# Triangular inverse of the delta rule in 32x32 blocks on four partition groups

## The reference, cut to what matters

```python
D_MODEL = 2048
SEQ = 256
DN_HEADS = 8
DN_HEAD_DIM = 128
DN_CHUNK = 64

def chunk_gated_delta_rule(q, k, v, g, beta):
    ...
    decay = jnp.exp(jnp.where(causal, g[..., :, None] - g[..., None, :], -jnp.inf))
    k_beta = k * beta[..., None]
    v_beta = v * beta[..., None]
    a = jnp.einsum("bhncd,bhnsd->bhncs", k_beta, k) * decay
    t_mat = jnp.eye(C, dtype=jnp.float32) + jnp.where(strict, a, 0.0)
    rhs = jnp.concatenate([v_beta, k_beta * jnp.exp(g)[..., None]], axis=-1)
    sol = lax.linalg.triangular_solve(t_mat, rhs, left_side=True, lower=True, unit_diagonal=True)
    ...
```

## Time and profile before

| | us |
|---|---|
| median of 3 runs | 2566.45 (2566.37 to 2567.07) |
| the profiled execution | 2566.27 |
| its span, first to last instruction | 2564.5 |
| TensorE busy | 2543.6 (99%) |
| VectorE busy | 1674.9 (65%) |
| ScalarE busy | 1339.4 (52%) |
| DMA, mean | 184 GB/s |

### The profile page before, as it was taken

One profiled execution on the slowest core, in us unless ns is written; L12 is line 12 of the kernel. 1 busy time (PEld: TensorE's weight loads), 2 busy tenths in 40 slices (PEclk: granted clock), 3 DMA queues, 4 the chain that ended last, 5 costly groups with the idle time before them and its releaser, 6 DMA issues.

```text
span 2564.5 us, 33902 instructions
## 1 busy us (share of the span) xinstructions
PE 2543.6 (99%) x13816; PEld 2149.8 (84%) x13816; DVE 1674.9 (65%) x2150; ACT 1339.4 (52%) x1893; POOL 0.2 (0%) x4
## 2 busy tenths in 40 slices
PE   9999999999999999999999999999999999999998
PEld 7878888888888888887888888888888888888887
DVE  7686566655665566668778987555566655665565
ACT  6565554444444446568766656544554444444444
POOL 0000000000000000000000000000000000000000
PEclk9999999999999999999999999999999999999999
DMA  6544666566556555555454447554656655655654
GB/s 226 166 138 145 223 222 202 188 196 192 189 195 191 189 195 178 189 184 171 144 181 147 149 149 253 175 166 153 197 181 197 197 185 193 195 185 195 196 187 143
DMA packets 235858, 470.79 MB, mean 184 GB/s; under 512 B 8283, under 2 KB 17206, under 8 KB 234550
## 3 DMA queue, kind: packets, MB, share of 16 engines
q1 hardware_dynamic: 234950, 467.04, 55.7%
q10 hardware_dynamic: 752, 1.58, 0.2%
HBM read 462.30 MB, written 6.29 MB: 183 GB/s over the span
## 4 chain that ended last, share of the span: by engine, by line
PE 49%; DVE 1%; ACT 1%; issue 0%; DVEq 0%
PE ps L1291 10%; PE ps L1293 10%; PE ps L1292 10%; PE ps L1330 9%; PE ps L1329 5%; PE ps L1679 1%; PE ps L1362 0%; ACT WH L1911 0%; PE ps L1829 0%; PE ps L1857 0%; PE ps L1828 0%; PE ps L1856 0%; PE ps L1855 0%; PE ps L1827 0%; PE ps L1662 0%
## 5 line engine op out<-in xcount | busy, mean ns | idle before, releaser
L2663 DVE TENSOR_TENSOR WL<-Wt,WH 128x1024 fp32r<-128x1024 f32 (+1 forms) x861 | 1037.9, 1210 | 678.1 <-ACT WH L1911 630.0
L1911 ACT ACTIVATE WH<-Wt 128x1024 fp32r<-128x1024 f32 (+1 forms) x861 | 895.4, 1047 | 777.6 <-PE ps L1293 517.6
L1291 PE MATMUL ps<-WH,XT 128*128 128x512 f32 (+1 forms) x1184 | 469.6, 397 | 0.8 <-DVE WL L2663 0.5
L1293 PE MATMUL ps<-WH,XT 128*128 128x512 f32 (+1 forms) x1184 | 459.5, 388 | 0.0
L1292 PE MATMUL ps<-WL,XT 128*128 128x512 f32 (+1 forms) x1184 | 459.2, 388 | 0.0
L1291 PE MATMUL ps<-WH,HT 128*128 128x512 f32 (+2 forms) x1176 | 456.1, 388 | 1.5 <-DVE WL L2663 1.5
L1293 PE MATMUL ps<-WH,HT 128*128 128x512 f32 (+2 forms) x1176 | 451.4, 384 | 0.0
L1292 PE MATMUL ps<-WL,HT 128*128 128x512 f32 (+2 forms) x1176 | 451.0, 384 | 0.0
L1330 PE MATMUL ps<-XT,WH 128*128 128x512 f32 x960 | 336.5, 394 | 0.0
L1330 PE MATMUL ps<-HT,WH 128*128 128x512 f32 x960 | 336.5, 394 | 0.0
L1329 PE MATMUL ps<-XT,WL 128*128 128x256 f32 x960 | 266.6, 278 | 0.0
(11 more groups left out here) (424 smaller groups left out, 1922.2 us busy)
## 6 DMA issues: line engine op xcount, KB each, us to landing
Wt<-in_mlp_w SPq DMA_DIRECT2D x128, 1024.0 KB, 5.2
Wt<-in_w_up SPq DMA_DIRECT2D x64, 1024.0 KB, 5.2
Wt<-in_w_down SPq DMA_DIRECT2D x64, 1024.0 KB, 5.0
Wt<-in_w_in SPq DMA_DIRECT2D x53, 1024.0 KB, 5.1
Wt<-in_w_out SPq DMA_DIRECT2D x32, 1024.0 KB, 5.1
Wt<-in_xa_wk SPq DMA_DIRECT2D x16, 1024.0 KB, 5.1
Wt<-in_xa_wv SPq DMA_DIRECT2D x16, 1024.0 KB, 5.1
Wt<-in_xa_wq SPq DMA_DIRECT2D x16, 1024.0 KB, 5.2
```

The lines of the kernel that those rows point to most:

```text
L1291: pe.matmul(o, xh, wh, start=start, stop=False)
L1293: done = pe.matmul(o, xl, wh, start=False, stop=stop)
L1911: act.activation(m.WH[:, i % NR, 0:2 * w], m.Wt[:, slot % NW, h * 2 * w:(h + 1) * 2 * w], ACT.Copy).then_inc(*up("wsplit.a", i))
L2663: dve.tensor_tensor(m.WL[:, i % NR, 0:2 * w], m.Wt[:, slot % NW, h * 2 * w:(h + 1) * 2 * w], m.WH[:, i % NR, 0:2 * w].bitcast(F32), SUB).t ...
```

## The change

Levels 0 to 4 of the inverse work inside blocks of 32, so four 32x32 blocks of a head can lie on four partition groups, `QUARTERS`, packed in 32 columns. `small_blocks` is that view: 8 heads x 32 columns, 256 in all. For li below 5, `on_tiles` issues 8 x 4 matmuls of 32x32; masks, factor and copies are 256 columns wide. `d_blocks` adds four copies of 32x256 on ScalarE into the upper part of MI and keeps the two wide ones, which only the mask of level 32 reads. After li = 4 VectorE spreads MI and MT back to 64-wide blocks, `widen`: the 32 columns are read twice and multiplied by `own32`. That replaces ScalarE's two copies there. The yield between `d_blocks` and `d_first` goes, and the second mask moves from `d_lev2` into `d_first`.

```diff
     for s in LEVELS:
-        r, c = (i, j) if s == LEVELS[-1] else (i % 64, j[:, 0:64])
+        w = P if s == LEVELS[-1] else max(2 * s, 32)
+        r, c = i % w, j[:, 0:w]
...
+    parts.append(("ident32", (i % 32 == j[:, 0:32]) * 1.0))
     parts.append(("ident64", (i % 64 == j[:, 0:64]) * 1.0))
+    parts.append(("own32", (i % 64 // 32 == j[:, 0:64] // 32) * 1.0))
...
+QUARTERS = tuple(slice(32 * n, 32 * n + 32) for n in range(4))
+
+def small_blocks(t, part=0):
+    return t[:, 2 * part:2 * part + 2, :].rearrange("p a (e c) -> p (a e) c", e=4)
...
             p.do("d_blocks", b)
-            yield
             p.do("d_first", b)
             yield
             yield
...
     def on_tiles(name, b, li, use, left, right):
+        tiles, w = (TILES, 64) if li == 5 else (QUARTERS, 32)
         for s in freed(use):
             on.wait_ge(*s)
         for h in range(8):
-            for r in TILES:
-                done = pe.matmul(m.bank(use)[r, 64 * h:64 * h + 64], left(r, h), right(r, h), start=True, stop=True)
+            for r in tiles:
+                done = pe.matmul(m.bank(use)[r, w * h:w * h + w], left(r, h), right(r, h), start=True, stop=True)
...
     def d_left(b, li, use):
+        part = blocks if li == 5 else small_blocks
         on.wait_ge(*at("delta.v", "level", b, li))
-        on.wait_ge(*at("delta.a", "plain", b, li - 1))
+        on.wait_ge(*(at("delta.v", "plain", b) if li == 5 else at("delta.a", "plain", b, li - 1)))
...
     def d_blocks(b):
         on.wait_ge(*at("delta.v", "pairs", b))
+        for r in QUARTERS:
+            act.activation(small_blocks(MI, 2)[r, :, :], AT[r, :, r], ACT.Copy).then_inc(*up("delta.a", "blocks", b))
         for r in TILES:
-            act.activation(blocks(MT, 1)[r, :, :], AT[r, :, r], ACT.Copy).then_inc(*up("delta.a", "blocks", b))
+            act.activation(blocks(MT, 1)[r, :, :], AT[r, :, r], ACT.Copy).then_inc(*up("delta.a", "wide blocks", b))
...
     def d_first(b):
         on.wait_ge(*at("delta.a", "blocks", b))
         delta_prev(b)
-        dve.tensor_tensor(blocks(BT), blocks(MT, 1), mk("lev1"), MUL).then_inc(*up("delta.v", "level", b, 0))
+        dve.tensor_tensor(small_blocks(BT), small_blocks(MI, 2), mk("lev1"), MUL).then_inc(
+            *up("delta.v", "level", b, 0))
         on.wait_ge(*at("delta.v", "level", b, 0))
-        dve.tensor_tensor(blocks(MT), mk("ident64"), blocks(BT), SUB).then_inc(*up("delta.v", "first", b))
-
-    @named
-    def d_lev2(b, use):
+        dve.tensor_tensor(small_blocks(MT), mk("ident32"), small_blocks(BT), SUB).then_inc(*up("delta.v", "first", b))
         on.wait_ge(*at("delta.v", "qk", b, 1))
         if b == 0:
             on.wait_ge(*at("delta.v", "dl"))
-        dve.tensor_tensor(blocks(DT), blocks(MT, 1), mk("lev2"), MUL).then_inc(*up("delta.v", "level", b, 1))
+        dve.tensor_tensor(small_blocks(DT), small_blocks(MI, 2), mk("lev2"), MUL).then_inc(*up("delta.v", "level", b, 1))
...
+    def widen(dst, use):
+        ps = m.bank(use)[:, 0:256].rearrange("p (h c) -> p h c", h=8)
+        own = m.cst("own32").rearrange("p (e c) -> p e c", e=2)
+        return dve.tensor_tensor(blocks(dst).rearrange("p h (e c) -> p h e c", e=2),
+                                 ps.unsqueeze(2).to_broadcast([P, 8, 2, 32]),
+                                 own.unsqueeze(1).to_broadcast([P, 8, 2, 32]), MUL)
...
     def d_right(b, li, turned, plain=None):
+        if li == 4:
+            on.wait_ge(*at("delta.t", "plain", b, 4))
+            widen(MI, plain).then_inc(*up("delta.v", "plain", b, frees=plain))
+            on.wait_ge(*at("delta.t", "turned", b, 4))
+            widen(MT, turned).then_inc(*up("delta.v", "turned", b, frees=turned))
```

More of the change, by code:

```diff
@@ L1684, in d_lev2 @@
         on.wait_ge(*at("delta.v", "first", b))
-        on_tiles("plain", b, 0, use, lambda r, h: blocks(MT)[r, h, :], lambda r, h: ident[r, r])
+        on_tiles("plain", b, 0, use, lambda r, h: small_blocks(MT)[r, h, :], lambda r, h: ident[r, r])
     @named
     def d_left(b, li, use):
+        part = blocks if li == 5 else small_blocks
         on.wait_ge(*at("delta.v", "level", b, li))
-        on.wait_ge(*at("delta.a", "plain", b, li - 1))
-        on_tiles("left", b, li, use, lambda r, h: blocks(bts[li % 2])[r, h, :], lambda r, h: blocks(MI)[r, h, :])
+        on.wait_ge(*(at("delta.v", "plain", b) if li == 5 else at("delta.a", "plain", b, li - 1)))
+        on_tiles("left", b, li, use, lambda r, h: part(bts[li % 2])[r, h, :], lambda r, h: part(MI)[r, h, :])
     @named
     def d_right(b, li, turned, plain=None):
+        part = blocks if li == 5 else small_blocks
         on.wait_ge(*at("delta.v", "factor", b, li))
-        on.wait_ge(*(at("delta.a", "turned", b, li - 1) if li > 1 else at("delta.v", "first", b)))
+        if li == 5:
+            on.wait_ge(*at("delta.v", "turned", b))
+        else:
+            on.wait_ge(*(at("delta.a", "turned", b, li - 1) if li > 1 else at("delta.v", "first", b)))
         if plain:
-            on_tiles("plain", b, li, plain, lambda r, h: blocks(MT)[r, h, :], lambda r, h: blocks(m.E0)[r, h, :])
-        on_tiles("turned", b, li, turned, lambda r, h: blocks(m.E0)[r, h, :], lambda r, h: blocks(MT)[r, h, :])
+            on_tiles("plain", b, li, plain, lambda r, h: part(MT)[r, h, :], lambda r, h: part(m.E0)[r, h, :])
+        on_tiles("turned", b, li, turned, lambda r, h: part(m.E0)[r, h, :], lambda r, h: part(MT)[r, h, :])
     @named
@@ L2436, in d_right @@
     def d_right(b, li, turned, plain=None):
-        if plain is None:
+        if li >= 4:
             return
@@ L3459, in d_left @@
         to, src = bts[(li + 1) % 2], AT
-        if LEVELS[li + 1] < 64:
+        if LEVELS[li + 1] == 32:
+            on.wait_ge(*at("delta.a", "wide blocks", b))
             to, src = blocks(to), blocks(MT, 1)
+        elif LEVELS[li + 1] < 32:
+            to, src = small_blocks(to), small_blocks(MI, 2)
         dve.tensor_tensor(to[:, :, :], src[:, :, :], mk(f"lev{LEVELS[li + 1]}"), MUL).then_inc(
```

5 lines of the change are left out of this document (3 added, 2 removed).

## The result

The changed kernel takes 2571.1 us (median of 13 runs, 2568.75 to 2574.84) against 2566.5 (2566.35 to 2567.07): ratio 1.0019, 95% interval 1.0011 to 1.0026. I had forecast 2554.4. It is a little slower, and its runs lie 6 us apart where those of before lie 0.7 apart. The profiled execution took 2568.9 us, span 2567.1, that is 2.6 us more than the span before.

What follows compares the result with a forecast made beforehand. TensorE, busy 99% of the span, was taken as the bound. Products -11.1 and waits -1.0 made -12.1 us: 2564.5 - 12.1 + 1.8 = 2554.2, 2554.4 at the median; range 2551 to 2582.

Steps and rivals of the forecast that it cites:

- Product term: Inverse's small matmuls, levels 0 to 4: 26 batches at 0.51 us, 0.42 to 0.43 less each, -11.1 us.
- 29 ns: Inverse batches: every record costs 29 ns whatever its width, 1.87 us a batch, 2587.8 us in all; chance 0.10.
- 25 ns: Inverse batches: starts on all tiles average at least 25 ns apart, 1.60 us a batch, 2581.5 us; chance 0.13.
- chained records: Inverse batches: only neighbouring instructions overlap, two at a time, 1.02 us a batch, 2567.5 us; shares chance 0.19.
- 0.83 ns a column and 5 ns a round: Inverse batches: line through 111 ns at 128 columns and 58 at 64, giving 32 ns a round at 32 columns.
- all on TensorE's path: Inverse batches: the whole -11.1 us from 26 shorter batches was claimed to shorten TensorE's time.
- four rivals: Inverse batches: records at 29 ns (0.10), starts 25 ns apart (0.13), chained pairs (0.19), half the gain at 10-12 ns (0.08).
- the move: Inverse's masks on VectorE's queue, one yield gone: TensorE's waits fall from 3.0 to 2.0 us, -1.0; bounds -3.0 and +2.
- the later WH and WL splits catch TensorE once more: Upper bound for the masks' new queue place: splits delayed on ScalarE and VectorE make TensorE wait, +2 us.
- Waits: TensorE in the inverse: mask waits of 0.77, 1.61, 0.63 go; level 1's factor costs 1.7 and 0.3; -1.0 us.
- Masks, copies, widen: VectorE and ScalarE in the inverse: 256-column masks and copies, two 0.68 us `widen` products; cost TensorE nothing.
- No change: Inverse batches: records chained in pairs or fed near 14 ns each, so time stays about the same; chance 0.19.

Runs made afterwards that it cites:

- the tiles alone: 32x32 tiles with every step in its old queue place (yield back, second mask in `d_lev2`), against the kernel before: 2566.1 us, ratio 0.9994.
- the burst of 32x32 matmuls: The changed kernel with the first batch of each b issued twelve times over: 2606.7 us in one run.
- the burst on 64x64 tiles: The kernel before with matmuls of levels 0 to 4 cut into two of 32 columns and each b's first batch issued twelve times: 2661.4 us, one run.

## Why the prediction was wrong

- *Product term.* Forecast 0.51 us a batch and -11.1; measured 0.56 and -10.2. Tiles do run apart, and all three rivals on pace fall for four tiles: 29 ns, 25 ns and chained records would make 1.87, 1.60 and 1.02 us. The floor of 25 ns between starts of the Trainium skill ("TensorE: Matmul & The Clock Gate", section "Wait — 56ns, not 53.3ns?") doesn't hold on four tiles: 62 starts in 0.58 us. Single starts in the trace of the kernel before were 6 to 7 and 51 to 52 ns apart in turn, so looking below the mean of 29 would have shown that two tiles are not bound by it. The reason that I gave was wrong, though: "0.83 ns a column and 5 ns a round". 32 columns on a 64x64 tile cost as much as 64. The line through two sizes gave nearly the right value because the tile shrank with the columns, which is luck.
- *The first step that failed* is the half sentence "all on TensorE's path" with no price for twice the instructions. I asked how fast a record runs once it is there, in four rivals, and not whether it is there: the queue of instructions itself, which the page of the profile lists in one row. That row (109 packets of 16,384 bytes) and the records between two packets would have given the question. The pauses took 5.2 us of the 10.2 in the profiled execution, and with half clock most of it in the median run of the tiles alone.
- *The second step that failed* is the move, forecast at -1.0 with the bound +2. I followed VectorE's queue from the masks to the factor, 12 us, and stopped there; "the later WH and WL splits catch TensorE once more" was the wrong mechanism and too small. The yield sits in a chain, so everything behind it moves, up to `d_out`, two halves earlier. The norm's wait (3.95) with its clock (1.4 to 1.6) cost more than 5 us, 5.1 and 5.2 by the two runs that put `d_out` back; the move is 7.7 in all on 64x64 tiles.
- *Waits.* Which would go and which would come in the inverse was right: one for level 1's factor of 1.7 + 0.3, measured 2.01 + 0.78; sum -0.2 for -1.0. What a wait does behind its end was not counted: the half-clock stretch, +1.4.
- *Masks, copies, widen.* No wait of TensorE for any of them, as forecast.
- *The sum.* The profiled execution lies 14.7 us above the 2554.2 forecast for it: product 0.9, waits 0.8, pauses 5.2, norm 3.95, clock 3.0, and 0.9 that is not explained but for the 0.4 at the start.
- *Range and chances.* 2551 to 2582 holds the time, by the width that the pace rivals gave it. The result is 4.6 us from no change, within the 5.1 that I had called the same, for a reason that none of my cases had. "No change" at 2567.5 came nearest, by chance.

## What to carry to other kernels

When a change trades long instructions for more short ones, count instructions per microsecond against what the queue's packets can bring (here 128 matmul records in 3.46 us, and in 4.3 to 6.8 with weights in transfer), and space dense groups with long work. When a step is moved in a chain, follow the chain to its last user: here an end two halves earlier and one six later both cost more than the step. Price an idle of TensorE of about 2 us with the half-clock stretch that may follow.

## What the runs showed of the hardware

- TensorE's instructions come in packets of 16,384 bytes, 128 matmul records with their weight loads. In the burst of 32x32 matmuls a packet starts 1.1 us after TensorE begins the one before, and TensorE goes on 2.36 us after that, 3.46 in all. Over all runs it is 3.2 to 4.0 us in ten pauses and 4.3 to 6.8 in the 24 with a weight transfer under way.
- Records of 32x32 on four tiles start 9 ns apart on average (62 in 0.58 us).
- On two 64x64 tiles a record takes 58 ns of its tile for 64 columns and for 32 (the run with halved columns).
- The granted clock fell to 0.50 (1.2 GHz), mostly for 3.4 us, behind some idles of 1.75 to 3.95 us and not behind others of 1.92 to 2.49 us. In the burst on 64x64 tiles it stayed there for 34.1 us while TensorE ran without a stop.
